# Later transposes behind the scores in four attentions, and two feed-forward weight panels split earlier on ScalarE

## The reference, cut to what matters

```python
s = jnp.where(valid, s, -jnp.inf)
m = jnp.maximum(jnp.max(s, axis=-1, keepdims=True), sk)
p = jnp.exp(s - m)
p = p / (jnp.sum(p, axis=-1, keepdims=True) + jnp.exp(sk - m))
o = jnp.einsum('bhgqj,bjhd->bqhgd', p.astype(v.dtype), v_c)
```

## Time and profile before

| | us |
|---|---|
| median of 3 runs (lowest to highest) | 2132.02 (2130.04 to 2132.17) |
| the profiled execution's own time | 2129.73 |
| its span | 2127.9 |
| TensorE busy | 2011.2 (95%) |
| VectorE, ScalarE, GpSimd busy | 997.5, 878.3, 698.5 |

### The profile page before, as it was taken

How to read it: one execution, slowest core, us unless ns; L and a number is a source line. 1 busy time by engine, 2 the same in 40 slices (tenths; PEclk the granted TensorE clock), 3 DMA queues, 4 the chain that set the end, 5 groups by cost and what they waited for, 6 DMA issues and landing times.

```text
span 2127.9 us, 28226 instructions
## 1 busy us (share of the span) xinstructions
PE 2011.2 (95%) x10632; PEld 1569.2 (74%) x10632; DVE 997.5 (47%) x1770; ACT 878.3 (41%) x1664; POOL 698.5 (33%) x394
## 2 busy tenths in 40 slices
PE   5999999999999999999899999999998899999998
PEld 3888655688665567887677888887885477888886
DVE  3520778523366653378437435343116625525254
ACT  4322667424376654534453222225225643323233
POOL 1322122342100045331234444443442334444433
PEclk9999999999999999998899999999999999999999
DMA  8222333132100012230125333322331122333332
GB/s 297 60 66 63 100 100 109 51 104 65 40 1 1 1 30 88 71 90 31 42 82 156 127 99 94 104 90 73 106 107 51 44 78 80 109 98 93 99 92 84
DMA packets 209467, 174.36 MB, mean 82 GB/s; under 512 B 6080, under 2 KB 180775, under 8 KB 208183
## 3 DMA queue, kind: packets, MB, share of 16 engines
q1 hardware_dynamic: 206096, 163.86, 25.4%
q0 software_dynamic: 2192, 8.45, 1.2%
q10 hardware_dynamic: 1047, 0.26, 0.1%
HBM read 170.41 MB, written 7.38 MB: 84 GB/s over the span
## 4 chain that ended last, share of the span: by engine, by line
PE 80%; issue 7%; DVE 6%; ACT 4%; POOL 2%; SPq 1%; DMA 0%; POOLq 0%; DVEq 0%; ACTq 0%
PE ps L369 20%; PE ps L370 20%; PE ps L371 20%; PE ps L745 5%; PE ps L626 4%; PE ps L709 3%; POOL WL L1613 1%; PE ps L607 1%; DVE PT L727 1%; PE ps L690 1%; ACT PB L661 1%; SPq L1507 1%; PE ps L1129 1%; PE ps L1228 1%; DVE PB L649 1%
## 5 line engine op out<-in xcount | busy, mean ns | idle before, releaser
L1613 POOL TENSOR_TENSOR WL<-raww,WH 128x1024 fp32r<-128x1024 f32 (+1 forms) x247 | 583.0, 2365 | 909.6 <-ACT WH L321 832.7
L369 PE MATMUL ps<-HH,WH 128*128 128x512 f32 (+1 forms) x1368 | 522.4, 382 | 16.6 <-DVE HL L2580 7.8
L370 PE MATMUL ps<-HL,WH 128*128 128x512 f32 (+1 forms) x1368 | 518.6, 379 | 0.0
L371 PE MATMUL ps<-HH,WL 128*128 128x512 f32 (+1 forms) x1368 | 518.2, 379 | 0.0
L321 ACT ACTIVATE WH<-raww 128x1024 fp32r<-128x1024 f32 (+1 forms) x247 | 254.8, 1036 | 416.0 <-PE ps L371 411.3
L369 PEld LDWEIGHTS ps<-HH,WH 128*128 128x128 f32 x1368 | 259.4, 190 | 73.3 <-issue 17.5
L371 PEld LDWEIGHTS ps<-HH,WL 128*128 128x128 f32 x1368 | 259.0, 189 | 48.6
L370 PEld LDWEIGHTS ps<-HL,WH 128*128 128x128 f32 x1368 | 259.5, 190 | 46.6
L709 PE MATMUL ps<-ident,PB 128*128 128x128 f32 x952 | 157.7, 284 | 31.3 <-ACT PB L661 22.7
L709 PEld LDWEIGHTS ps<-ident,PB 128*128 128x128 f32 x952 | 109.4, 143 | 60.0 <-ACT PB L661 35.5
L661 ACT ACTIVATE PB<-PB,NB 128x512 f32<-128x512 f32 (+3 forms) x192 | 116.5, 607 | 73.1 <-DVE NB L649 70.2
(11 more groups left out here) (346 smaller groups left out, 3130.8 us busy)
## 6 DMA issues: line engine op xcount, KB each, us to landing
raww<-in_ffn_w_up SPq DMA_DIRECT2D x88, 512.0 KB, 3.8
raww<-in_ffn_w_down SPq DMA_DIRECT2D x40, 512.0 KB, 3.4
raww<-in_ada_w SPq DMA_DIRECT2D x32, 512.0 KB, 3.6
raww<-in_odd_w_in SPq DMA_DIRECT2D x24, 512.0 KB, 3.7
raww<-in_a_w_in SPq DMA_DIRECT2D x20, 512.0 KB, 3.8
raww<-in_even_w_in SPq DMA_DIRECT2D x17, 512.0 KB, 3.8
ADA<-in_ada_w SPq DMA_DIRECT2D x6, 1024.0 KB, 16.2
raww<-in_b_w_in SPq DMA_DIRECT2D x12, 512.0 KB, 3.9
```

Of the source, the lines that this page charges most:

```text
L369: nc.tensor.matmul(out, lh, rh, start=start and k == ks[0], stop=False)
L370: nc.tensor.matmul(out, lh, rl, start=False, stop=False)
L371: ins = nc.tensor.matmul(out, ll, rh, start=False, stop=stop and k == ks[-1])
L1613: nc.gpsimd.tensor_tensor(lo, raw_slot(k), hi.bitcast(F32), ALU.subtract).then_inc(*split_lo.mark(k))
```

## The change

The distance between a tile's scores and its transposes becomes a number, `lag`: 3 in A and B, 4 in E and O. `PB` gets six slots of 512 columns in E and O (the same memory), four of 768 stay in A and B. Value products and `keep_o` follow the lag by default (`lag + 1`); in A the plan for the first pair of heads of each group of four becomes (5, 3). Reciprocal and spread stay where they were. In `ffn_act` the panels after slice 0 go up to v0 + 6, those after slice 1 up to v1 + 5.

```diff
-        PB = over("PB", 0, 4 * R)[:, :].rearrange("p (t n) -> p t n", n=R)
+        PBF = over("PB", 0, 4 * R)[:, :]
+        def prob(A, t):
+            w = 4 * R // A["slots"]
+            n = t % A["slots"]
+            return PBF[:, n * w:(n + 1) * w]
 in att_max and att_exp:
-            if t >= 4:
-                q, j = A["seq"][t - 4]
+            if t >= A["slots"]:
+                q, j = A["seq"][t - A["slots"]]
...
 in att_pe, att_dve and att_act:
-                q, j = att_at(A, t - 2)
+                q, j = att_at(A, t - A["lag"])
...
 in finish_att:
-            A.setdefault("pv_plan", lambda r: (3, 4))
+            A.setdefault("lag", 2)
+            A.setdefault("slots", 4)
+            A.setdefault("pv_plan", lambda r: (A["lag"] + 1, 4))
...
-                late, over_ = A["pv_plan"](r) if r + 1 < len(jobs) else (3, 1)
+                late, over_ = A["pv_plan"](r) if r + 1 < len(jobs) else (A["lag"] + 1, 1)
...
 ATT_A:
-                                      "pv_plan": lambda r: (3, 4) if r % 4 == 1 else (5, 2),
+                                      "lag": 3,
+                                      "pv_plan": lambda r: (5, 3) if r % 4 == 1 else (5, 2),
 ATT_B:
+                            "lag": 3
 ATT_E and ATT_O:
+                                      "lag": 4, "slots": 6,
...
 in ffn_act:
                     ahead(act, ("up_u", l, i), 3)
                     gelu(i)
                     high(i)
-                    ahead(act, ("up_v", l, i), 3)
+                    ahead(act, ("up_v", l, i), {0: 6, 1: 5}.get(i, 3))
```

More of the change, by code:

```diff
@@ L641, in att_max @@
                 return
-            if t >= 4:
-                q, j = A["seq"][t - 4]
+            if t >= A["slots"]:
+                q, j = A["seq"][t - A["slots"]]
                 dve.wait_ge(*turned[A["name"], q, j, len(A["jobs"][q]["tiles"][j]["lots"]) - 1])
-            dst, src = PB[:, t % 4, 0:job["tiles"][i]["n"] * P], score_span(A, r, i)
+            dst, src = prob(A, t)[:, 0:job["tiles"][i]["n"] * P], score_span(A, r, i)
             if len(add.shape) == 3:
@@ L656, in att_exp @@
             fused = job["tiles"][i]["add"] is not None
-            if t >= 4 and not fused:
-                q, j = A["seq"][t - 4]
+            if t >= A["slots"] and not fused:
+                q, j = A["seq"][t - A["slots"]]
                 act.wait_ge(*turned[A["name"], q, j, len(A["jobs"][q]["tiles"][j]["lots"]) - 1])
-            dst = PB[:, t % 4, 0:job["tiles"][i]["n"] * P]
+            dst = prob(A, t)[:, 0:job["tiles"][i]["n"] * P]
             nc.scalar.activation(dst, dst if fused else score_span(A, r, i), ACT.Exp, bias=NB[:, r % 4, i:i + 1],
@@ L709, in att_turn @@
                     ins = nc.tensor.transpose(ps[:, b, q * P:(q + 1) * P],
-                                              PB[:, t % 4, (first + q) * P:(first + q + 1) * P], ident[:, :])
+                                              prob(A, t)[:, (first + q) * P:(first + q + 1) * P], ident[:, :])
                 ins.then_inc(*turned.mark(*key))
@@ L1161, in build @@
                                       "kept": lambda p: (dve_out, ("a scaled",) + p),
-                                      "fill_pe": a_fill_pe, "fill_dve": a_fill_dve, "per": 4, "gate": a_gate,
+                                      "fill_pe": a_fill_pe, "fill_dve": a_fill_dve, "per": 4, "lag": 3, "gate": a_gate,
                                       "pt": lambda r: ((0, 0), (2, 0), (1, 0), (1, C))[r % 4],
                                       "pt_free": lambda r: (r - 4) | 1,
-                                      "pv_plan": lambda r: (3, 4) if r % 4 == 1 else (5, 2),
+                                      "pv_plan": lambda r: (5, 3) if r % 4 == 1 else (5, 2),
                                       "bc": BCA, "bc_free": lambda r: gated["A", r],
@@ L1358, in build @@
                             "prep_pe": b_prep_pe, "prep_act": b_prep_act, "prep_dve": b_prep_dve,
-                            "score_wait": b_wait})
+                            "score_wait": b_wait, "lag": 3})
         ATT_B["high_at"] = {ATT_B["steps"] - 1: 15}
@@ L1410, in build @@
         ATT_E = both_prep(finish_att({"name": "E", "jobs": e_jobs(), "scale": HD ** -0.5, "keep_o": e_keep,
-                                      "per": 2, "paired": True, "single": True,
+                                      "per": 2, "paired": True, "single": True, "lag": 4, "slots": 6,
                                       "pt": lambda r: ((4, 2, 5, 6)[r % 4], 0), "pt_free": lambda r: (r - 4) | 1, "bc": BC, "bc_free": lambda r: o_made["E", (r // 2, "lat")], "q": e_q, "k": e_k, "q2": e_q2, "kh": e_kh, "kl": e_kl}))
@@ L1483, in build @@
                             "kept": lambda p: (dve_out, ("o scaled", p[0])) if p[0] < 7 else (o_made, ("O", p)),
-                            "prep_act": o_prep_act, "prep_dve": o_prep_dve, "paired": True, "single": True,
+                            "prep_act": o_prep_act, "prep_dve": o_prep_dve, "lag": 4, "slots": 6, "paired": True, "single": True,
                             "pt": lambda r: ((4, 2, 5, 6)[r % 4], 0), "pt_free": lambda r: (r - 4) | 1,
```

## The result

| | before | after |
|---|---|---|
| median (lowest to highest), us | 2132.06 (2130.04 to 2132.17), 4 runs | 2144.48 (2141.74 to 2148.61), 4 runs |
| ratio, 95% interval | | 1.0061 (1.0049 to 1.0073) |
| profiled execution, span | 2129.73, 2127.9 | 2143.51, 2141.7 |

The changed kernel is slower by 0.6%. Forecast were 2115 us and, with 0.87, a faster one. (The kernel before ran a fourth time beside it, so its median is not the 2132.02 of above.) The two spans differ by 13.8 us. To see where, each stage is split at instants that both traces have: "scores" is the time from the first to the last score product of an attention, "end" the time from there to the first product L369 of the projection behind it. The instants are read to about 0.3 us, in all kernels alike.

What follows compares the result with a forecast made beforehand. TensorE, busy 95% of the span, was taken as the bound. Terms -8 - 4 - 2 + 0 - 3 = -17 from 2129.73 gave 2112.7, plus 2.3: 2115 us; range 2108 to 2122 (chance 0.60), outer 2102 to 2131.

Steps and rivals of the forecast that it cites:

- O, -8: Attention O, lag 2 to 4: transposes stop waiting for the exponential, 1.0 of 1.44 us gained in each of 8 pairs.
- Feed-forward, -3: Two feed-forward layers: earlier panels remove TensorE's waits for POOL's low part, 1.5 us a layer; bounds -4 and +2.
- A, -2: Attention A, lag 2 to 3: copy wait of 4.5 us goes, 2.4 us comes in at bank 7; bounds -5 and +4.
- B, 0: Attention B, lag 2 to 3: scores still wait for their banks, value products move later at no cost; bounds -4 and +4.
- E, -4: Attention E, lag 2 to 4: pairs gain 5 us, the end costs 1 us; bounds -18 and +6.
- the wait moving to the spread: Rival: spread waits for the reciprocal instead; a third of O's and E's gain stays, A gives nothing; 2125 us, chance 0.14.
- +3: E's end: cost in us by the port-pair rule, with the scaling moved into POOL's stretch; the forecast kept +1.
- The slower rival: E and O: scaling stacked on the reciprocal at a pair's start blocks scores behind the spread; +8, 2140 us, chance 0.07.
- The clock rival: E and O: TensorE, waiting less, stays at the high clock, 11 us more gained; 2104 us, chance 0.14.

Runs made afterwards that it cites:

- The second experiment: Kernel before with only A's long-pair value-product plan changed from (3, 4) to (5, 3), except the last group, lag 2 kept: 2147.35 us, A 194.6 + 7.2.
- The fourth experiment: Changed kernel with A and B as before, and E's scaling one step later, behind the next pair's reciprocal, at lag 4: 2118.55 us, E 36.8 + 15.7.

## Why the prediction was wrong, step by step

The forecast named three signs of being wrong. Two came: A got longer, and E's end cost more than its pairs gave. The third, a pair of O above 10.4 us, did not.

- **O, -8: near in size** (-9.5), **and partly by luck.** The exponential's wait went, but the wait at the spread took its place at 0.94 us a pair, not the 0.44 that the sum left. Between the two pairs at full clock the gain is 10.73 - 9.95 = 0.78 us for the 1.0 taken; eight times that is 6.2 us. The rest fits the clock, which rose from 0.93 to 0.98 over O and of which the forecast had counted nothing: 92.9 x 0.05 x 2 = 9 us less at the low level, by an estimate up to 4.6 us. The two errors cancel; no run parts them.
- **Feed-forward, -3: right** (-3.4), with one wait of 0.5 us left.
- **A, -2: this step failed** (+14.9, of which the scores 13.1). It asked what waits for what (the copy, bank 7) and found a margin for each, and it put the move of the products themselves at nothing. It didn't ask which work fills TensorE while VectorE is the slower of the two. The value products were that filler in the short pair's steps; (5, 3) leaves none of them there, and they lengthen the long pairs instead (125.6 us for 114.6). The margin at bank 7 was right (L750 waits 1.1 us for L1086) and beside the point. The second experiment shows the plan as the cause, without the lag. The lag by itself, at the same plan but for the last group, is worth 5.4 us at (5, 3) and 0.2 at (4, 4), in single runs. Part of the loss is the low clock that came with it, up to 8 us by the estimate above.
- **B, 0: failed in small** (+3.5). Its products moved one step later (from z + 3 to z + 4; the forecast's "steps 4 to 7" should have been 3 to 6), and the forecast gave this move no price. One step costs 6.3 us, the lag returns 3.3. That products finished earlier gain 8.5 shows that their place in B was never indifferent. Which wait carries the 6.3 us was not followed.
- **E, -4: failed in both halves.** The pairs were to give 5 and gave -0.4. The forecast named the cause as a rival, the wait moving to the spread, and priced it at a third of the gain kept; none was kept, and the first spreads wait 2.3 us each. The fourth experiment gets 5.3 us against before by moving the scaling behind the reciprocal, which is the forecast's 5. The end was to cost +1 and cost +7.8. The argument for +1, that nothing on TensorE waits for that scaling at once, overlooked that the reciprocal is queued behind it on VectorE; the spread waits 7.75 us for it. The Trainium skill's rule on the port pair that was weighed there (SBUF — State Buffer, "SBUF: two separate sides") gave the right kind, and +3 was too little: blocked were not only the cast and the subtraction but the sum behind them. Holding POOL back until the reciprocal takes 4.8 us off the end, the later scaling alone 1.8; with both, and POOL behind the scaling, the end is 9.4 to 9.8 us, as before.
- **The slower rival** (2140 us, 0.07) had its mechanism in E, not in O, and a price that fits only by chance: over half of the 26.6 us comes from A, which it did not contain. A and E passed their upper bounds (+14.9 for +4, +8.2 for +6). All upper bounds together, +21, would have held the result, but the outer range ended at 2131. A bound from the work moved would have been larger for A: its value products moved out of VectorE's full steps leave TensorE idle there, 5.61 - 3.67 = 1.9 us a short pair in the window above, for 7 such pairs 13.6 us, an estimate from one window.
- **The clock rival** (2104 us, 0.14) came true in O alone. In E the clock fell from 0.78 to 0.64, where the forecast looked for 0.8 to 0.95, and A lost its 1.00.

## What to carry to other kernels

Before a step of a software pipeline is moved, ask of each interval which engine is the slower one there and what fills the other: work that hides behind VectorE in one step is on the path in the next, though no semaphore wait is added. In E a longer lag needed the consumer behind it in the queue (the scaling) moved past the reciprocal as well; without that its gain turned into a wait one link on. In O the lag paid without it, and in B shorter plans paid more than any lag. And where VectorE's work shifts in time, look for GpSimd's bulk work in the place it shifts to.

## What the hardware showed that was not expected

- Low clock in a stage that had none: A's mean went from 1.00 to 0.96, with 0.72 behind an idle stretch of 1.85 us and 0.50 in the plan-only kernel behind one of 1.53; there the same product group is slow as well as late (2.77 and 3.68 us for 1.51). A place that makes TensorE idle was paid for a second time in the next steps. It isn't so each time: lag 3 with (4, 4) has idle stretches of 1.85 and 2.00 us in the same places and a mean of 0.99.
- The same program of E at 36.9 and 40.0 us in two kernels that differ only in B, beside a lower granted clock; the two other kernels with B's short plans had 39.5 and 40.0, the three others with this E and B's longer ones 36.8 or 36.9.
- A sum of 128x8 floats at 2.30 us and a cast of 128x512 at 2.13 us beside GpSimd's subtractions, for 0.16 and 0.43 us without them.
- B gains 8.5 us when its value products come in two pieces instead of four, and 11 us in one. That VectorE's wait for B's scores falls from 63.1 to 55.2 us fits; why TensorE passes the lump more cheaply than four small pieces is open. Four pieces one step later cost 6.3 us, which fits that being done early counts; whether fewer pieces count by themselves was not parted from it.
